# A hybrid decoder trunk on one core: output product added by halves, five column steps moved behind the first scores, key digits in one batch, first gather issued alone

## The chip, the cores and the metric

The kernel runs on 1 core of one Trainium2 chip. The metric is the device time of one execution in microseconds (us), median over runs.

## The reference, cut to what matters

```python
DEPTH, SEQ, D_MODEL = 2, 256, 1024
PEER_HEADS, PEER_TOPK, N_KEYS = 8, 16, 128
for layer in range(DEPTH):
    h = rms_norm(x, norm_mix[layer])
    z = h @ w_in[layer]                     # 1024 x 2564 columns
    ...                                     # four groups of heads: forgetting, dilated,
    ...                                     # differential attention, S5 state space model
    x = x + mixed @ w_out[layer]            # "the output product"
    h = rms_norm(x, norm_ffn[layer])
    q = (h @ wq).reshape(c, 8, 2, 128)      # queries
    sc = einsum('thpd,hpkd->thpk', q, keys) # scores against 128 keys, two sides
    top_v, top_i = top_k(sc, 16)            # per head and side
    cand = top_v[..., 0, :, None] + top_v[..., 1, None, :]      # 256 pairs
    best_v, best_pos = top_k(cand, 16)
    ids = 128 * top_i[side 0][best_pos >> 4] + top_i[side 1][best_pos & 15]
    act = gelu(einsum('td,thkd->thk', h, peer_u[ids])) * softmax(best_v)
    x = x + einsum('thk,thkd->td', act, peer_v[ids])
```

For each of 256 tokens, 128 rows of `peer_u` and 128 of `peer_v` are fetched by number in each layer.

## The kernel before, in words

The 256 tokens are two blocks of 128, and there are two layers, so the work is four passes n = 0 to 3 (layer n // 2, block n % 2). A pass has the mixing part (columns of `w_in`, heads, S5, output product, queries, scores, search for the best pairs) and the part that gathers. Each pass gathers 128 slots: slot t is one indirect DMA of GpSimd (L1724) that brings for each of 128 tokens one row of 2048 float32, the row of u and of v side by side: 1.05 MB. 512 slots in all are 538 of the 630 MB moved.

The gathered rows land in `ring`, which has 10 places. Work goes in groups of four slots. For group i VectorE makes four dot products ("dots", L1301), ScalarE a gelu, VectorE the weights ("weigh", L1310), ScalarE four diagonal matrices (L820), and TensorE four products that sum the rows of v in PSUM ("rows of v", L1669). When TensorE has used a slot (`v_used`), GpSimd may gather the next one into the same place.

The mixing part of pass n + 1 is spread between the groups of pass n. A list of names (`plan_steps`) sets the order of all steps; each engine walks that same list and does its own share of each step, in that order, with semaphores between engines. Before the first group of pass 0 stands the list `first`: there the mixing part of pass 0 has nothing to hide behind.

Names in `first` that the change touches. "out 0" to "out 3" are the output product (L1614). "out" on VectorE adds it to x (L1160). "rows 1" transposes x (L1371) and scales it into `hT` (VectorE L940 for one half, ScalarE L666 for the other). "query 4" and "score 4" are the first half of the queries and scores of quarter 0, from which "quick 0" on VectorE finds the first eight slots' ids (L1169 to L1189) and releases GpSimd by `quick_ready`. "best", "pairs" and "ids" are the full search; "ids" turns positions into row numbers (L1264 to L1286). "query 5", "query 1", "query 2" and "query 3" follow on TensorE (L1636). "next columns 0" to "7" are eight steps of the columns of block 2 (pass 1), 512 and 256 columns wide (L1434). Their input lies in ring places 4 to 6, so a gather to these places waits for `z_ps` of 8, the last of them. The weights of queries 1, 2 and 3 lie in places 8 and 9, 0 and 1, 2 and 3; so slots 4, 6 and 8 (with 5, 7 and 9 behind them) wait for `qT_ps`, the queries. Slot 10 and all later ones wait for `v_used`.

The heads, the S5 scan ("turn on"), "y" (L1573, L1574), "gate rows" (L1581) and "glu" (L1588) come ahead of the output product.

Of the kernel before, what the change touches and what calls it, by code (L numbers as in the profile page):

```python
# [8 lines left out]
ALU = mybir.AluOpType  # L9
# [6 lines left out]
P = 128  # L16
D = 1024
# [21 lines left out]
FIRST_PLACE = 4  # L39
# [92 lines left out]
def plan_steps():  # L132
# [32 lines left out]
    def do(names, n):  # L165
        for name in names:
# [3 lines left out]
            else:  # L170
# [18 lines left out]
             ["next columns 6", "rows 1", "next columns 7", "next z", "square 1", "gain", "query 4", "mean 1", "score 4"],  # L189
             ["quick 0", "best 4", "pairs 4", "query 5", "score 5", "query 1", "score 1", "ids 4", "query 2", "score 2", "best 5", "pairs 5",]]  # L190
# [49 lines left out]
def trunk(nc, x_in, w_in, w_out, row_in, gain_ffn, s5_in, glu_w, peer_wq, keys_t, table_uv,  # L240
          rel_bias, const_in, bucket_in, out):
    ctx = ExitStack()
    with ctx:
# [87 lines left out]
        posf, idf = T[:, 640:768], [T[:, 768:896], T[:, 896:1024]]  # L331
# [3 lines left out]
        hit = T[:, 2048:2560].rearrange("p (n k a) -> p n k a", k=TOPK, a=TOPK)  # L335
        v16_kept, i16_kept = by(last_keys[:, 0:64], TOPK), by(last_keys[:, 64:128].bitcast(U32), TOPK)
        late_cand = by(T[:, 4096:4352], 2 * P)
        late_hit = T[:, 4608:4864].rearrange("p (n k a) -> p n k a", k=TOPK, a=TOPK)
        late_best, late_pos = by(T[:, 4864:4896], TOPK), by(T[:, 4896:4928].bitcast(U32), TOPK)
        late_posd, late_posf, late_i16f = T[:, 4928:4960].bitcast(U32), T[:, 4960:4992], by(T[:, 4992:5056], TOPK)  # L340
        late_idf = [T[:, 5056:5088], T[:, 5088:5120]]
# [62 lines left out]
        gain_ps, mT_ps, mT_dve, mT_act, wo_ps, x_ready = sem("gain_ps"), sem("mT_ps"), sem("mT_dve"), sem("mT_act"), sem("wo_ps"), sem("x_ready")  # L404
        head_q_ps, head_qT, head_sc, cst_rest = sem("head_q_ps"), sem("head_qT"), sem("head_sc"), sem("cst_rest")
# [423 lines left out]
        def _(v):  # L829
# [326 lines left out]
            def out_rows(n, i):  # L1156
                if i == 3:
                    b = n % NB
                    v.wait_ge(wo_ps, n + 1)
                    v.tensor_tensor(x[:, b, :], x[:, b, :], ps[:, 2:4, :].rearrange("p c n -> p (c n)"), ALU.add).then_inc(x_ready, 1)  # L1160

            def quick(n, i):
# [3 lines left out]
                slots, hits = slice(0, 8), hit[:, 0, 0:8, 0:8]  # L1166
# [4 lines left out]
                for k in range(2):  # L1171
                    step.free(v.max_index(i16[:, k, 0:8], v16[:, k, 0:8], scores[k]))
                step(v.tensor_tensor(by(sums, 8), bc(v16[:, 0, 0:8], 2, 8), bc(v16[:, 1, 0:8], 1, 8), ALU.add))
                step(v.max(best[:, 0, 0:8], sums))
                step.free(v.tensor_copy(i16f[:, 0:2, 0:8], i16[:, 0:2, 0:8]))
                step(v.max_index(pos[:, 0, 0:8], best[:, 0, 0:8], sums))
                pos_f = pos.rearrange("p n k -> p (n k)")[:, slots]
                for s in range(2):
                    if s == 0:
                        step(v.tensor_single_scalar(posd[:, slots], pos_f, 3, op=ALU.logical_shift_right))  # L1180
                    else:
                        step(v.tensor_single_scalar(posd[:, slots], pos_f, 7, op=ALU.bitwise_and))
                    step(v.tensor_copy(posf[:, slots], posd[:, slots]))
                    step(v.tensor_tensor(hits, bc(posf[:, slots], 2, 8), bc(cst[:, C_IOTA:C_IOTA + 8], 1, 8), ALU.is_equal))
                    step(v.tensor_tensor(hits, hits, bc(i16f[:, s, 0:8], 1, 8), ALU.mult))
                    step(v.reduce_sum(idf[s][:, slots], hits, AX))
                step(v.scalar_tensor_tensor(out=idf[0][:, slots], in0=idf[0][:, slots], scalar=float(NK), in1=idf[1][:, slots],
                                            op0=ALU.mult, op1=ALU.add))
                v.tensor_copy(ids[:, 0, slots], idf[0][:, slots]).then_inc(quick_ready, 1)  # L1189
                v.wait_ge(quick_ready, 1)  # L1190
# [60 lines left out]
            def find_ids(n, i):  # L1251
# [9 lines left out]
                hits = hit[:, 0:count, :, :]  # L1261
                hit3 = hits.rearrange("p n k a -> p (n k) a")
# [563 lines left out]
```

## Time and profile before

| | us |
|---|---|
| median of 3 runs | 1578.69 (1577.34 to 1579.03) |
| the profiled execution's own time | 1583.69 |
| its span | 1581.9 |

In the profile, PE is TensorE's matmuls, PEld its weight loads, DVE VectorE, ACT ScalarE, POOL GpSimd, SP SyncE. A row of the timeline gives start, length, engine, line, what it writes and reads, how many instructions were merged, and in brackets the idle time before it with what ended it. PEclk is the granted TensorE clock as a share of full speed. GB/s is what the DMA engines moved in a stretch.

### The profile page before, as it was taken

To read this page: it belongs to the slowest core of one execution; us is meant where nothing else is said; L and a number is where in the kernel's file an instruction comes from. 1 tells how busy PE (TensorE), PEld (TensorE's weight loads), DVE (VectorE), ACT (ScalarE), POOL (GpSimd) and SP (SyncE) were. 2 spreads that over 40 slices of the span, in tenths; PEclk is the share of its full clock that TensorE was granted. 3 is DMA by queue.
4 is the path that set the end of the run, shared out by engine and by line. 5 is a ranking of instruction groups with operands and counts; after the bars stand their busy time and mean duration, and the time that the engine had idled before them with its cause. 6 is when DMAs were issued, how large, how long until landed. Compare 5 with 4: busy or idle time off the path is not lost.

```text
span 1581.9 us, 15174 instructions
## 1 busy us (share of the span) xinstructions
PE 1366.8 (86%) x4622; PEld 741.3 (47%) x4622; DVE 1173.6 (74%) x2848; ACT 455.0 (29%) x1095; POOL 608.3 (38%) x525
## 2 busy tenths in 40 slices
PE   8998999999695997988888799999969787788777
PEld 4766455554472444443356345455437433333333
DVE  6828999788698887874569788886658987665554
ACT  3522144443212234342122134343212222121112
POOL 1003355345334334553434333545434434333331
PEclk9999999999898999998989899999989889989999
DMA  9648999999999999999999999999999999999997
GB/s 360 269 164 347 389 380 422 406 402 421 423 421 421 422 398 422 422 419 423 423 410 409 422 423 420 417 384 403 422 423 419 388 408 422 422 419 421 422 421 300
DMA packets 87517, 629.97 MB, mean 398 GB/s; under 512 B 9825, under 2 KB 11105, under 8 KB 16910
## 3 DMA queue, kind: packets, MB, share of 16 engines
q0 software_dynamic: 74144, 537.97, 82.6%
q1 hardware_dynamic: 13294, 91.05, 14.1%
q8 instruction: 38, 0.62, 0.2%
q14 instruction: 41, 0.34, 0.1%
HBM read 627.91 MB, written 1.06 MB: 398 GB/s over the span
## 4 chain that ended last, share of the span: by engine, by line
PE 43%; DMA 29%; DVE 18%; issue 7%; ACT 3%; POOL 1%; SPq 0%; DVEq 0%; ACTq 0%
DMA ring<-table_uv,ids 28%; PE ps L1669 24%; DVE ring L1301 6%; PE ps L1636 5%; PE ps L1449 3%; PE ps L1412 2%; PE ps L1614 1%; ACT acts L797 1%; ACT diag L820 1%; PE ps L1516 1%; PE ps L1680 1%; POOL ring L1724 1%; DVE W L1276 1%; DVE W L1274 1%; DVE W L1277 1%
## 5 line engine op out<-in xcount | busy, mean ns | idle before, releaser
L1669 PE MATMUL ps<-ring,diag 128*128 128x512 f32 x1884 | 890.0, 627 | 194.3 <-ACT diag L820 185.4
L1724 POOL DMA_INDIRECT ring<-table_uv,ids x512 | 602.7, 1177 | 939.1 <-PE ps L1669 779.4
L1669 PEld LDWEIGHTS ps<-ring,diag 128*128 128x128 f32 x1884 | 370.7, 201 | 663.6 <-issue 652.0
L1301 DVE CUSTOM_DVE_ANT_0 ring<-ring,h 128x1024 f32<-128x1024 f32 x384 | 455.2, 1223 | 139.9 <-DMA ring<-table_uv,ids 137.9
L797 ACT ACTIVATE acts<-dots,small 128x4 f32<-128x4 f32 x126 | 37.5, 297 | 876.3 <-DVE dots L1301 850.3
L1301 DVE CUSTOM_DVE_ANT_0 ring<-ring,ps 128x1024 f32<-128x1024 f32 x120 | 144.6, 1220 | 97.7 <-DMA ring<-table_uv,ids 97.5
L820 ACT ACTIVATE diag<-cst,weights 128x128 f32<-128x128 f32 x471 | 151.4, 390 | 28.9 <-DVE weights L1310 27.8
L1449 PE MATMUL ps<-W,hT 128*128 128x512 f32 (+2 forms) x256 | 95.2, 527 | 2.7 <-DVE hT L940 2.7
L1636 PEld LDWEIGHTS ps<-hT,W 128*128 128x128 f32 x832 | 94.5, 192 | 3.3 <-issue 3.3
L1636 PE MATMUL ps<-hT,W 128*128 128x128 f32 x832 | 95.3, 275 | 0.0
L1449 PEld LDWEIGHTS ps<-W,hT 128*128 128x128 f32 x256 | 48.5, 190 | 52.0 <-issue 47.4
L1614 PE MATMUL ps<-W,hT 128*128 128x512 f32 x128 | 57.3, 593 | 0.8 <-DVE hT L1154 0.8
L797 ACT ACT_TABLE_LOAD x43 | 55.2, 1283 | 4.8 <-DVE dots L1301 4.0
L1310 DVE TENSOR_TENSOR weights<-acts,gates 128x4 f32<-128x4 f32 x126 | 20.6, 163 | 47.4 <-ACT acts L797 46.3
L1317 DVE SCALAR_TENSOR_TENSOR x<-ring,weights,x 128x1024 f32<-128x1024 f32 x33 | 42.4, 1285 | 1.4 <-DVE weights L1310 0.2
L1301 DVE DVE_READ_ACCUMULATOR2_ANT dots<- 128x1 f32 x504 | 41.2, 82 | 0.0
L1614 PEld LDWEIGHTS ps<-W,hT 128*128 128x128 f32 x128 | 23.9, 190 | 29.2 <-issue 28.2
L1516 PE MATMUL ps<-W 128*128 128x256 f32 (+1 forms) x128 | 32.9, 340 | 2.8 <-DVE h L1121 1.4
L1089 DVE TENSOR_REDUCE small<-ps 128x4 f32<-128x512 f32 (+1 forms) x16 | 15.3, 953 | 23.0 <-PE ps L1523 11.6
L728 ACT ACTIVATE W<-ps,small 128x128 f32<-128x128 f32 (+1 forms) x64 | 26.0, 418 | 15.4 <-DVE small L1090 15.3
L1516 PEld LDWEIGHTS ps<-W 128*128 128x128 f32 x128 | 22.2, 198 | 8.3 <-issue 5.8
L1526 PE MATMUL ps<-bias,cst 128*128 128x128 f32 (+1 forms) x96 | 24.6, 339 | 0.0
(316 smaller groups left out, 1190.8 us busy)
## 6 DMA issues: line engine op xcount, KB each, us to landing
W<-peer_wq SPq DMA_DIRECT2D x11, 2048.0 KB, 19.7
W<-w_in SPq DMA_DIRECT2D x16, 1282.0 KB, 11.6
W<-w_out SPq DMA_DIRECT2D x7, 2048.0 KB, 11.2
ring<-table_uv,ids POOLq DMA_INDIRECT x512
W<-w_in SPq DMA_DIRECT2D x8, 898.0 KB, 8.8
ring<-peer_wq SPq DMA_DIRECT2D x3, 2048.0 KB, 21.0
W<-w_in SPq DMA_DIRECT2D x4, 1024.0 KB, 11.5
ring<-w_in SPq DMA_DIRECT2D x2, 1544.0 KB, 20.3
```

The source lines that it names most:

```text
L728: a.activation(pbuf[:, i, 0:nk], lg[:, i * nk:(i + 1) * nk], ACT.Exp, bias=small[:, 72 + i:73 + i], accum_out=small[:, 80 + i:81 + i]).the ...
L797: a.activation(acts[:, g * RING_G:(g + 1) * RING_G], dots[:, g * RING_G:(g + 1) * RING_G], ACT.Gelu_apprx_tanh, scale=ffn_rstd[n % NB]).th ...
L820: a.activation(diag[:, s, :], ident, ACT.Copy, scale=weights[:, s:s + 1]).then_inc(diag_ready, 1)
L1301: v.tensor_tensor_reduce(ring_u[:, r, :], ring_u[:, r, :], tokens, 1.0, 0.0, ALU.mult, ALU.add, dots[:, s:s + 1]).then_inc(dots_done, 1)
L1317: v.scalar_tensor_tensor(out=x[:, b, :], in0=ring_v[:, r, :], scalar=weights[:, s:s + 1], in1=x[:, b, :], op0=ALU.mult, op1=ALU.add).then_ ...
L1412: mm = pe.matmul(ps[:, z_bank(0, bank), 0:c1 - c0], hT[:, k, :], first_at[group][:, k, a0:a0 + c1 - c0], start=(k == 0), stop=(k == KC - 1))
L1449: mm = pe.matmul(ps[:, 2 + i, 0:c1 - c0], hT[:, k, :], win_at(n)[:, slot, c0:c1], start=(k == 0), stop=(k == KC - 1))
L1516: pe.matmul(dst, q, k, start=True, stop=False)
L1614: mm = pe.matmul(ps[:, 2 + c, :], hT[:, k, :], half[:, k % 4, c * 512:(c + 1) * 512], start=(k == 0), stop=(k == KC - 1))
L1636: mm = pe.matmul(ps[:, 6 + q % 2, i * P:(i + 1) * P], wq_at(n, q)[:, k, i * P:(i + 1) * P], hT[:, k, :], start=(k == 0), stop=(k == KC - 1))
L1669: mm = pe.matmul(ps[:, c, :], diag[:, s, :], ring_v[:, r, c * 512:(c + 1) * 512], start=(k == 0), stop=(k == SLOTS - 1), skip_group_check= ...
L1724: gp.indirect_dma_start(ring[:, place(t), :], None, table_uv, bass.IndirectOffsetOnAxis(ap=ids[:, b, k:k + 1], axis=0)).then_inc(pair_in[p ...
```

## The change

Five things. First, in pass 0 the last step of the output product does its two chunks of 512 columns one after the other. VectorE adds each half to x when it is there (`wo_half`, `x_half`), TensorE transposes the first four blocks of x after the first half, `rows_half` releases VectorE's scaling, and the first query starts on `hT`'s first half. Second, "next columns 3" to "7" and "next z" move behind "score 4"; "next columns 2" moves to where 4 was. Third, both digits of a position (side 0 and side 1) are made by one batch of instructions of double width, in "quick" and in all "ids" steps. Fourth, the id of slot 0 is written as soon as the best key of each side is known, and its gather goes to place 7, which waits only for `glu_ps`. Fifth, other slots of the first four wait for the second increment of `quick_ready` and for `z_ps` as before.

```diff
-FIRST_PLACE = 4
+PLACES = (7, 4, 5, 6, 8, 9, 0, 1, 2, 3)
...
-             ["keys 2", "next columns 2", "weights 2", "heads 1", "next columns 3", "inverse 2"],
+             ["keys 2", "weights 2", "heads 1", "inverse 2"],
              ["heads 2", "logits 6", "co sums"],
-             ["logits 7", "y 0", "next columns 4", "softmax 3", "co scale"],
-             ["weights 3", "y 1", "next columns 5", "s5 out", "inverse 3"],
+             ["logits 7", "y 0", "next columns 2", "softmax 3", "co scale"],
+             ["weights 3", "y 1", "s5 out", "inverse 3"],
...
-             ["next columns 6", "rows 1", "next columns 7", "next z", "square 1", "gain", "query 4", "mean 1", "score 4"],
-             ["quick 0", "best 4", "pairs 4", "query 5", "score 5", "query 1", "score 1", "ids 4", "query 2", "score 2", "best 5", "pairs 5",]]
+             ["rows 1", "square 1", "gain", "query 4", "mean 1", "score 4"],
+             ["quick 0", "next columns 3", "next columns 4", "next columns 5", "next columns 6", "next columns 7", "next z", "best 4", "pairs 4", "query 5", "score 5", "query 1", "score 1", "ids 4", "query 2", "score 2", "best 5", "pairs 5",]]
...
+                    if n == 0:
+                        v.wait_ge(wo_half, 1)
+                        v.tensor_tensor(x[:, b, 0:512], x[:, b, 0:512], ps[:, 2, :], ALU.add).then_inc(x_half, 1)
+                        v.wait_ge(wo_ps, 1)
+                        v.tensor_tensor(x[:, b, 512:D], x[:, b, 512:D], ps[:, 3, :], ALU.add).then_inc(x_ready, 1)
+                        return
...
+                v.scalar_tensor_tensor(out=ids[:, 0, 0:1], in0=i16f[:, 0, 0:1], scalar=float(NK), in1=i16f[:, 1, 0:1],
+                                       op0=ALU.mult, op1=ALU.add).then_inc(quick_ready, 1)
...
-                for s in range(2):
-                    if s == 0:
-                        step(v.tensor_single_scalar(posd[:, own], pos_f, 4, op=ALU.logical_shift_right))
-                    else:
-                        step(v.tensor_single_scalar(posd[:, own], pos_f, TOPK - 1, op=ALU.bitwise_and))
-                    step(v.tensor_copy(posf[:, own], posd[:, own]))
-                    step(v.tensor_tensor(hit3, bc(posf[:, own], 2, TOPK),
-                                         bc(cst[:, C_IOTA:C_IOTA + TOPK], 1, TOPK * count), ALU.is_equal))
-                    step(v.tensor_tensor(hits, hits, bc(i4[:, :, s, :], 2, TOPK), ALU.mult))
-                    step(v.reduce_sum(idf[s][:, own], hit3, AX))
...
+                step.free(v.tensor_single_scalar(digit[:, :, 0, :], at, 4, op=ALU.logical_shift_right))
+                step(v.tensor_single_scalar(digit[:, :, 1, :], at, TOPK - 1, op=ALU.bitwise_and))
+                step(v.tensor_copy(posf[:, two], posd[:, two]))
+                step(v.tensor_tensor(hit3, bc(posf[:, two], 2, TOPK), bc(cst[:, C_IOTA:C_IOTA + TOPK], 1, 2 * TOPK * count), ALU.is_equal))
+                step(v.tensor_tensor(hits, hits, bc(i16f[:, keys, :], 2, TOPK), ALU.mult))
+                step(v.reduce_sum(idf[:, two], hit3, AX))
...
+                if n // NB:
+                    step(v.tensor_scalar(low, low, float(NE * (n // NB)), None, ALU.add))
+                v.scalar_tensor_tensor(out=dst, in0=high, scalar=float(NK), in1=low, op0=ALU.mult, op1=ALU.add).then_inc(ids_ready, 1)
...
+                order = [(k, c) for k in range(OUT_CUTS[i], OUT_CUTS[i + 1]) for c in range(2)]
+                if n == 0 and i == 3:
+                    order.sort(key=lambda kc: kc[1])
...
+                        if n == 0 and part[0] == 0 and part[-1] == 1 and (i, k) == (0, KC // 2):
+                            pe.wait_ge(rows_act, 8)
...
+                        if t == 1:
+                            gp.wait_ge(quick_ready, 2)
...
                         elif t == 0:
+                            gp.wait_ge(glu_ps, 1)
+                        elif t == 1:
                             gp.wait_ge(z_ps, 8)
```

TensorE, from the output product (L1614 before, L1633 in the changed kernel) to the second half of the first queries. In the kernel before (L1434 is a column step's two products, L1371 the transposes of x, L1636 queries, L1652 scores):

```order
L1614 MATMUL ps<-W,hT 128x512 x12
L1434 MATMUL ps<-ring,diag 128x512
L1434 MATMUL ps<-ring,diag 128x256
L1371 MATMUL ps<-cst,x 128x128 x8
L1434 MATMUL ps<-ring,diag 128x512
L1434 MATMUL ps<-ring,diag 128x256
L1636 MATMUL ps<-hT,W 128x128 x16
L1652 MATMUL ps<-key_rows,h 128x128 x2
```

The same place in the changed kernel, where column steps are L1451, transposes L1388, queries L1660 and scores L1676:

```order
L1633 MATMUL ps<-W,hT 128x512 x12
L1388 MATMUL ps<-cst,x 128x128 x8
L1660 MATMUL ps<-hT,W 128x128 x16
L1676 MATMUL ps<-key_rows,h 128x128 x2
L1451 MATMUL ps<-ring,diag 128x512
L1451 MATMUL ps<-ring,diag 128x256
```

The two column steps left the way to the first scores, and behind those scores the last pair of rows stands five times in a row before the queries go on.

VectorE, the search for the first slots' ids ("quick"). In the kernel before, from the digit of side 0 to the ids:

```order
L1180 TENSOR_SCALAR W<-W 128x8
L1183 CAST W<-W 128x8
L1184 TENSOR_TENSOR W<-W,cst 128x8x8
L1185 TENSOR_TENSOR W<-W 128x8x8
L1186 TENSOR_REDUCE W<-W 128x8
L1182 TENSOR_SCALAR W<-W 128x8
```

The same search in the changed kernel, from the end of the search in the two score lists:

```order
L1185 CAST W<-W 128x2x8
L1186 SCALAR_TENSOR_TENSOR ids<-W 128x1
L1188 TENSOR_TENSOR W<-W 128x64
L1189 MAX W<-W 128x8
L1190 MAX_INDEX W<-W 128x8
L1192 TENSOR_SCALAR W<-W 128x8
L1193 TENSOR_SCALAR W<-W 128x8
L1194 CAST W<-W 128x16
L1196 TENSOR_TENSOR W<-W,cst 128x128
L1197 TENSOR_TENSOR W<-W 128x128
L1198 TENSOR_REDUCE W<-W 128x16
L1199 SCALAR_TENSOR_TENSOR ids<-W 128x7
```

The id of slot 0 is now written second of these rows, and the cast, compare, multiply and sum that stood once for each side stand once.

GpSimd, its first gathers with their waits, in the kernel before:

```order
L1724 DMA ring<-table_uv,ids 128x2048 [waits z_ps,quick_ready]
L1724 DMA ring<-table_uv,ids 128x2048 x3
L1724 DMA ring<-table_uv,ids 128x2048 [waits qT_ps]
```

And in the changed kernel:

```order
L1752 DMA ring<-table_uv,ids 128x2048 [waits glu_ps,quick_ready]
L1752 DMA ring<-table_uv,ids 128x2048 [waits z_ps,quick_ready]
L1752 DMA ring<-table_uv,ids 128x2048 x2
L1752 DMA ring<-table_uv,ids 128x2048 [waits qT_ps]
```

The first gather no longer waits for the column steps; the second one does.

## Rows read from the trace of the kernel before

**Rows 1.** The page's span and DMA total.
```profile
span 1581.9 us, 15174 instructions
DMA packets 87517, 629.97 MB, mean 398 GB/s; under 512 B 9825, under 2 KB 11105, under 8 KB 16910
```

**Rows 2.** Stretches: length, busy us (count) per engine, granted clock, DMA share, GB/s.
```profile
78.00:82.00 4.00, 4.00 (x16) 2.74 (x15) 1.31 (x5) 2.52 (x9) 0.00 (x0) 0.57 0.00 0
160.00:175.00 15.00, 12.70 (x30) 5.44 (x30) 14.39 (x54) 1.57 (x5) 8.77 (x7) 1.00 0.90 334
212.00:224.00 12.00, 12.00 (x31) 5.50 (x31) 11.15 (x23) 7.96 (x15) 7.58 (x6) 1.00 0.81 300
285.00:360.00 75.00, 69.33 (x256) 40.33 (x255) 61.37 (x145) 34.34 (x77) 33.22 (x27) 0.95 1.00 403
360.00:580.00 220.00, 189.48 (x664) 103.53 (x663) 179.83 (x476) 51.32 (x117) 88.78 (x72) 0.94 1.01 422
580.00:600.00 20.00, 19.52 (x54) 9.53 (x53) 18.88 (x45) 12.73 (x25) 8.47 (x7) 1.00 0.93 375
1240.00:1300.00 60.00, 43.16 (x80) 18.07 (x81) 53.55 (x159) 12.96 (x33) 22.74 (x22) 0.83 0.99 390
```

**Rows 3.** Timeline of GpSimd: slots 0, 1, 8, 14 and 30.
```profile
117.39 1.02 POOL L1724 DMA_INDIRECT ring<-table_uv,ids  x1 [96.49 <-DVE ids L1189]
118.71 0.97 POOL L1724 DMA_INDIRECT ring<-table_uv,ids  x1 [0.30 <-issue]
...
143.06 0.94 POOL L1724 DMA_INDIRECT ring<-table_uv,ids  x1 [5.51 <-PE ps L1636]
...
160.21 0.94 POOL L1724 DMA_INDIRECT ring<-table_uv,ids  x1 [7.59 <-PE ps L1669]
...
214.40 1.75 POOL L1724 DMA_INDIRECT ring<-table_uv,ids  x1 [6.74 <-PE ps L1669]
```

**Rows 4.** Timeline of TensorE, from the heads to the first rows of v.
```profile
71.05 1.51 PE L1434 MATMUL ps<-ring,diag 128*128 128x512 f32 x4
72.39 1.00 PE L1563 MATMUL ps<-zkv,W 128*128 128x64 f32 x8
...
75.78 0.49 PE L1516 MATMUL ps<-W 128*128 128x128 f32 x2 [1.44 <-DVE h L1121]
...
93.07 10.46 PE L1614 MATMUL ps<-W,hT 128*128 128x512 f32 x24
103.37 1.45 PE L1434 MATMUL ps<-ring,diag 128*128 128x512 f32 x4
...
107.28 3.81 PE L1636 MATMUL ps<-hT,W 128*128 128x128 f32 x32
...
112.17 3.74 PE L1636 MATMUL ps<-hT,W 128*128 128x128 f32 x32
...
143.97 6.60 PE L1669 MATMUL ps<-ring,diag 128*128 128x512 f32 x15
```

**Rows 5.** Timeline of VectorE: adds, searches, digits, and dots of group 1.
```profile
73.76 1.23 DVE L1079 TENSOR_TENSOR W<-W 128x1024 f32<-128x1024 f32 x1
...
103.57 1.22 DVE L1160 TENSOR_TENSOR x<-x,ps 128x1024 f32<-128x1024 f32 x1 [13.98 <-PE ps L1614]
...
112.37 0.50 DVE L1169 MAX8 W<-ps 128x8 f32<-128x128 f32 x2 [2.77 <-PE ps L1652]
...
122.40 0.17 DVE L1270 TENSOR_SCALAR W<-W 128x16 uint32<-128x16 uint32 x1
...
122.81 0.43 DVE L1274 TENSOR_TENSOR W<-W,cst 128x256 f32<-128x256 f32 x1
...
126.59 0.17 DVE L1284 TENSOR_REDUCE small<-gates 128x1 f32<-128x16 f32 x1
...
150.58 1.23 DVE L1301 CUSTOM_DVE_ANT_0 ring<-ring,h 128x1024 f32<-128x1024 f32 x1
...
183.21 0.69 DVE L1274 TENSOR_TENSOR W<-W,cst 128x512 f32<-128x512 f32 x1
```

More of the change, by code:

```diff
@@ L1165, in quick @@
                 sums = cand[:, 0, 0:64]
-                slots, hits = slice(0, 8), hit[:, 0, 0:8, 0:8]
+                slots, two = slice(0, 8), slice(0, 16)
+                hits = hit[:, 0:128].rearrange("p (s k a) -> p s k a", s=2, k=8)
+                digit = posd[:, two].rearrange("p (s k) -> p s k", s=2)
                 v.wait_ge(head_sc, 1)
@@ L1187, in quick @@
[L1187 to L1190, printed above, removed]
+                step.free(v.tensor_single_scalar(digit[:, 0, :], pos_f, 3, op=ALU.logical_shift_right))
+                step(v.tensor_single_scalar(digit[:, 1, :], pos_f, 7, op=ALU.bitwise_and))
@@ new lines, in quick @@
+                step(v.tensor_copy(posf[:, two], posd[:, two]))
+                hit3 = hits.rearrange("p s k a -> p (s k) a")
+                step(v.tensor_tensor(hit3, bc(posf[:, two], 2, 8), bc(cst[:, C_IOTA:C_IOTA + 8], 1, 16), ALU.is_equal))
+                step(v.tensor_tensor(hits, hits, bc(i16f[:, 0:2, 0:8], 2, 8), ALU.mult))
+                step(v.reduce_sum(idf[:, two], hit3, AX))
+                v.scalar_tensor_tensor(out=ids[:, 0, 1:8], in0=idf[:, 1:8], scalar=float(NK), in1=idf[:, 9:16],
+                                       op0=ALU.mult, op1=ALU.add).then_inc(quick_ready, 1)
@@ L1278, in find_ids @@
-                step(v.scalar_tensor_tensor(out=idf[0][:, own], in0=idf[0][:, own], scalar=float(NK), in1=idf[1][:, own],
-                                            op0=ALU.mult, op1=ALU.add))
-                step(v.tensor_scalar(idf[0][:, own], idf[0][:, own], float(NE * (n // NB)), None, ALU.add))
-                rest = slice(8, TOPK) if i == 4 else part
-                v.tensor_copy(ids[:, b, rest], idf[0][:, own if late else rest]).then_inc(ids_ready, 1)
+                at = by(pos_f, TOPK)
@@ L1283, in find_ids @@
+                step(v.reduce_sum(idf[:, two], hit3, AX))
+                k0 = 8 if i == 4 else 0
+                dst = by(ids[:, b, part], TOPK)[:, :, k0:TOPK]
+                high, low = found[:, :, 0, k0:TOPK], found[:, :, 1, k0:TOPK]
+                if n // NB:
+                    step(v.tensor_scalar(low, low, float(NE * (n // NB)), None, ALU.add))
+                v.scalar_tensor_tensor(out=dst, in0=high, scalar=float(NK), in1=low, op0=ALU.mult, op1=ALU.add).then_inc(ids_ready, 1)
                 v.wait_ge(gate_exp, found_ids(n, i))
@@ L1610, in out_rows @@
                     pe.wait_ge(wout_low_load, 16 * (n + 1))
-                for k in range(OUT_CUTS[i], OUT_CUTS[i + 1]):
-                    half = wout_halves[k // 4]
-                    for c in range(2):
+                order = [(k, c) for k in range(OUT_CUTS[i], OUT_CUTS[i + 1]) for c in range(2)]
+                if n == 0 and i == 3:
+                    order.sort(key=lambda kc: kc[1])
+                for k, c in order:
+                        half = wout_halves[k // 4]
                         mm = pe.matmul(ps[:, 2 + c, :], hT[:, k, :], half[:, k % 4, c * 512:(c + 1) * 512], start=(k == 0), stop=(k == KC - 1))
+                        if n == 0 and (k, c) == (KC - 1, 0):
+                            mm.then_inc(wo_half, 1)
                 if i == 3:
```

50 lines of the change are left out of this document (28 added, 22 removed).

## The prediction

> **What bounds the kernel now.** I read the total first. The span moves 630 MB [rows 1], and in a long undisturbed stretch the DMA engines move 422 GB/s (360 to 580 [rows 2]). 630 MB at 422 GB/s are 1493 us of a span of 1581.9. So the time is these 1493 us plus the time in which the DMA engines move less than they could, 89 us. An edit can save time only if it takes away some of this shortfall; an edit that shortens an engine's work while DMA is full buys nothing.
>
> Then the stretches. The shortfall of a stretch is its length times (1 - GB/s / 422). It is 3.1 us at 160 to 175, 3.5 us at 212 to 224, 3.4 us at 285 to 360, 2.2 us at 580 to 600 and 4.6 us at 1240 to 1300 [rows 2]. The rest lies before 160 or at the very end.
>
> Third, the timeline of GpSimd. The first gather starts at 117.39, when "quick" has written its ids, and slot 1 at 118.71. But slot 8 starts only at 143.06, released by the queries (L1636), and by then DMA had run dry. Slots 14 and 30 start at 160.21 and 214.40, both after a wait for TensorE's products of the rows of v (L1669) of 7.59 and 6.74 us [rows 3]. These two waits are the shortfalls at 160 to 175 and 212 to 224. In them VectorE is busy 14.39 of 15 us and 11.15 of 12, and TensorE all of the 12 [rows 2]. So from about 143 to 224 the engines are late and DMA waits for them; before 143 the slots wait for the queries.
>
> This gives two clocks to keep. The **DMA clock** is when slot 8 can start, since what was gathered before it has landed. The **engine clock** is when VectorE and TensorE do their groups. The later of the two sets the gathers up to 224.
>
> **The change part by part.**
>
> Up to the end of the output product (103.53 = 93.07 + 10.46 [rows 4]). Column steps leave TensorE here: a step costs 1.34 us, from 71.05 to 72.39 [rows 4]. Steps 3 and 2 leave a place where VectorE is the one waited for: the next logits on TensorE start at 75.78 after 1.44 us of idle time, released by VectorE [rows 4]. They save nothing there. Step 5 stood ahead of the last heads and saved time is possible, about 1 us. Against it stands the clock. It already falls, to a mean of 0.57 at 78 to 82 [rows 2], that is to the lower level of 1.2 GHz for most of that stretch, right after those 1.44 us of idle time, and the change makes that idle time about 1.3 us longer. A lower clock some 3 us earlier would slow the logits and "y", both on the way, by 1 to 2 us. Between -1.0 and +1.0 us, I take **0**.
>
> The Trainium skill ("TensorE: Matmul & The Clock Gate", Part 1) says that the idle state is the throttled one and that activity releases it, which speaks against taking matmuls out of a thin stretch; the trace agrees in that the only low clock between 60 and 104 comes behind the idle time. By the page alone this term would be +1.
>
> From the end of the product to the first scores: 112.37 - 103.53 = 8.84 us today [rows 4, 5]. In it lie the add of 1.22 us, eight transposes, the scaling and 3.81 us of queries [rows 4, 5]. New: the first half's add is done under the last products. The second half's add, of half the width, costs 0.69, by the row of 512 elements [rows 5]; it starts 0.05 after the product, and the first four transposes lie under it. From there: the other transposes 0.55, ScalarE's four scalings 1.15, then 28 of 32 query instructions, 3.81 × 28/32 = 3.3, less the first four that are waited for (24 of 32: 2.85), and 1.28 from the queries' end to the scores' use (112.37 - 107.28 - 3.81). Sum 0.05 + 0.7 + 0.6 + 1.2 + 2.85 + 1.28 = 6.7. Saved: **2.2 us**. The bounds are the removed half add alone (0.5) and all of the add and half the scaling (3).
>
> Five column steps now stand between "score 4" and "query 5": 5 × 1.34 = **6.7 us** on TensorE. Two of them had been covered, by VectorE's add and by the scaling; two or three by VectorE's scan. Nothing covers them now, because query 5 started at 112.17 [rows 4], at the very time of the scores. Queued behind them are queries 5, 1, 2 and 3, and slots 4 to 9 wait for these. So the DMA clock moves by 6.7 - 2.2 + 0 = **+4.5 us** (slot 8 from 143.06 to 147.6). Low end 3.5, high end 5.5 by the term above. The early gathers buy nothing: slot 0 starts some 5.3 us earlier than today, since "quick" writes it 1.6 us after its start where all eight took 5.0 (117.39 - 112.37 [rows 3, 5]), and slots 1 to 3 wait for the last column step, at about 117. Both are dry long before slot 8.
>
> The engine clock. VectorE: scores 2.2 earlier. "quick" loses four small instructions and two of 64 elements become one of 128: 0.7. "ids 4" takes from 122.40 to 126.59, 4.19 us [rows 5]. New: two digits and a cast at 0.2, less an overlap of 0.1, three instructions of 512 elements at 0.69 + 0.04 instead of six of 256 at 0.43 + 0.03, one ending instruction at 0.2 instead of three: 2.9. Saved 1.3, and 1.3 again in "ids 5". Group 1's dots, at 150.58 today [rows 5], can so start 5.5 us earlier; its four slots, 4 to 7, land 4.5 later than today, at about 146, which still fits. So group 1 is weighed some 5 us earlier. TensorE: the rows of v of group 0 move from 143.97 [rows 4] to 148.5, those of group 1 can follow without a gap, at about 156.4, and slot 14 is released near 158. DMA, with slots 8 to 13 in hand, runs dry at 160.2 + 4.5 = 164.7. **No shortfall at 160 to 175: -3.1.** TensorE then goes on without a gap, about 4.0 us ahead of today, because VectorE's group 2 ends 5 us ahead and its row scaling waits less. So slot 30 is released at 210.4. DMA, now 4.5 - 3.1 = 1.4 us behind today, runs dry at about 215. **No shortfall at 212 to 224: -3.5.** Sum by 224: +4.5 - 6.6 = -2.1.
>
> Later passes. An "ids" step with two heads changes six instructions of 512 elements (0.69 + 0.03) into three of 1024 (1.23 + 0.03 [rows 5]) and loses two or three small ones: 1.1 to 1.3 us each, 12 such steps. Where DMA is full that is nothing. It counts where DMA falls short and VectorE is late. At 1240 to 1300 VectorE is busy 53.6 of 60 us [rows 2], with two ids steps in it or right before: -1.4. At 580 to 600 TensorE is busy 19.5 of 20, so little: -0.3. At 285 to 360 the two late steps lie near the end: -0.3. Sum **-2.0**, between 0 (if the shortfalls are TensorE's) and -4.
>
> Total: 4.5 - 6.6 - 2.0 = **-4.1 us**. The sum is made against the profiled execution, 1583.69 (its span and 1.8 us around it), which stands 5.0 above the median of the runs; I carry the difference over to the median: 1578.69 - 4.1 = **1574.6**.
>
> **The rivals.** About 0.2% (3.2 us) is what this measurement can tell from no change.
>
> *A. The forecast*, the late start paid back by full DMA afterwards: 1574.6, chance 0.48.
>
> *B. The second shortfall stays.* TensorE has no gap at 212 to 224 [rows 2], so it alone could hold slot 30, if its lead is used up by waits on late slots. Then 4.5 - 3.1 - 2.0 = -0.6: 1578.1. For it: TensorE's own start of the rows of v is 4.5 us later. Against: the gap ahead of group 1 is longer than that. Chance 0.24.
>
> *C. Slower: the late queries are not paid back.* The place is slots 4 to 9. If the dots of groups 1 and 2 then wait for slots that land 4.5 us later, the releases of slots 14 and 30 move later with them, and both shortfalls stay: +4.5 - 1 (ids) = +3.5, 1582.2. It decides once less than 1.3 us of the 6.6 comes back. Against it: VectorE is busy 14.39 of 15 us at 160 to 175, so it is work and not arrivals that it is late by. Chance 0.13.
>
> *D. More.* The output product comes 1 us earlier, the clock holds, and the lead over DMA also closes part of 285 to 360 (2 of 3.4): 3.5 - 6.6 - 4.2 = -7.3, 1571.4. Chance 0.15.
>
> **How the numbers follow.** A's own range is 1572.5 to 1576.5. The range over all reaches to D and stops short of the worst of C: 1570.8 to 1580.0. Faster by over 0.2% is below 1575.5: most of A (0.38) and D (0.15), 0.53. Slower by over 0.2% is above 1581.9: half of C and a tail, 0.11. The rest, 0.36, is no change.
>
> **What would show it.** In the changed kernel's profile: slot 0 near 112 and slot 1 near 117; slot 8 near 147.5 (DMA clock); 422 GB/s from there past 224 with no dip at 160 to 175 and 212 to 224; group 1's dots near 145; clock below 1 some 3 us earlier than at 78 (the term of 0). It would be wrong if slot 8 comes later than 149, which means another TensorE wait behind the columns, or if GpSimd still waits some 6 us for slots 14 and 30 with DMA dry.

## The result, and the profile after

The changed kernel is slower: median of 5 runs 1587.19 us (1583.19 to 1592.63), against 1578.69 (1576.12 to 1580.8) for the kernel before in the same session. The ratio is 1.0051, with a 95% interval of 1.0033 to 1.007. Predicted were 1574.6 us and a range of 1570.8 to 1580.0. Two runs of more than 3500 us in the last set of experiments (one of the kernel before, one of the kernel before with both ids early) are in the medians of the table below and not in its ratios.

The profiled execution of the changed kernel took 1583.7 us, near the lowest of its runs; one that was profiled later took 1585.81. The kernel before was profiled at 1583.69, five above its median. So the two spans are equal by chance, and the stages must be read one by one. The page, its span and DMA totals, which answer to [rows 1]:

```profile
span 1581.9 us, 15072 instructions
DMA packets 87516, 629.97 MB, mean 398 GB/s; under 512 B 9825, under 2 KB 11105, under 8 KB 16910
```

The stretches of [rows 2] in the changed kernel, with the same columns:

```profile
78.00:82.00 4.00, 4.00 (x26) 3.20 (x26) 0.09 (x1) 2.34 (x6) 0.00 (x0) 0.81 0.00 0
160.00:175.00 15.00, 12.69 (x28) 5.25 (x28) 14.32 (x60) 1.57 (x5) 7.28 (x6) 0.95 0.90 341
212.00:224.00 12.00, 12.00 (x32) 5.57 (x31) 10.19 (x19) 7.10 (x14) 6.79 (x5) 1.00 0.83 328
285.00:360.00 75.00, 70.40 (x263) 41.07 (x262) 61.27 (x137) 35.60 (x80) 33.85 (x29) 0.98 1.00 406
580.00:600.00 20.00, 20.00 (x57) 9.93 (x56) 18.65 (x46) 13.48 (x28) 7.28 (x6) 1.00 0.93 359
1240.00:1300.00 60.00, 45.63 (x90) 19.03 (x91) 53.05 (x155) 12.96 (x33) 25.45 (x24) 0.89 1.00 400
```

Both dips that were to vanish are there: 341 GB/s at 160 to 175 is still 2.9 us short of 422, and 328 at 212 to 224 is 2.7 us short. GpSimd's timeline, the slots of [rows 3] and slot 1:

```profile
109.34 1.02 POOL L1752 DMA_INDIRECT ring<-table_uv,ids  x1 [88.29 <-DVE ids L1186]
114.69 0.97 POOL L1752 DMA_INDIRECT ring<-table_uv,ids  x1 [4.34 <-PE ps L1451]
...
144.63 0.94 POOL L1752 DMA_INDIRECT ring<-table_uv,ids  x1 [5.51 <-DVE ids L1293]
...
161.86 0.94 POOL L1752 DMA_INDIRECT ring<-table_uv,ids  x1 [7.66 <-PE ps L1693]
...
215.98 1.75 POOL L1752 DMA_INDIRECT ring<-table_uv,ids  x1 [6.81 <-PE ps L1693]
```

Slots 8, 14 and 30 are all later than in [rows 3], by 1.57, 1.65 and 1.58 us. From slot 8 on, the whole pattern has moved by one amount, that of the queries. TensorE, answering to [rows 4]:

```profile
71.04 0.39 PE L1543 MATMUL ps<-bias,cst 128*128 128x128 f32 x2
73.75 0.49 PE L1533 MATMUL ps<-W 128*128 128x128 f32 x2 [2.32 <-DVE h L1124]
...
90.07 10.46 PE L1633 MATMUL ps<-W,hT 128*128 128x512 f32 x24
...
107.29 6.62 PE L1451 MATMUL ps<-ring,diag 128*128 128x512 f32 x20
113.75 3.73 PE L1660 MATMUL ps<-hT,W 128*128 128x128 f32 x32
...
157.93 8.80 PE L1693 MATMUL ps<-ring,diag 128*128 128x512 f32 x16 [4.49 <-ACT diag L820]
```

The last row is the rows of v of group 1. They still wait 4.49 us for ScalarE's diagonals, as in the kernel before; the prediction had this gap gone. The row of before:

```profile
156.36 8.80 PE L1669 MATMUL ps<-ring,diag 128*128 128x512 f32 x16 [4.49 <-ACT diag L820]
```

Why it stayed is seen on VectorE ("ids 4", answering to [rows 5]) and on ScalarE at the same time:

```profile
107.50 0.50 DVE L1180 MAX8 W<-ps 128x8 f32<-128x128 f32 x2 [2.81 <-PE ps L1676]
...
116.50 0.17 DVE L1278 TENSOR_TENSOR gates<-W 128x16 f32<-128x16 f32 x1
...
119.63 0.17 DVE L1293 SCALAR_TENSOR_TENSOR ids<-W 128x8 uint32<-128x8 f32 x1
128.16 0.17 DVE L1295 TENSOR_REDUCE small<-gates 128x1 f32<-128x16 f32 x1 [8.36 <-ACT gates L783]
...
152.16 1.22 DVE L1312 CUSTOM_DVE_ANT_0 ring<-ring,h 128x1024 f32<-128x1024 f32 x1
```

```profile
125.91 0.60 ACT L776 ACTIVATE zkv<-ps 128x512 f32<-128x512 f32 x1 [8.01 <-PE ps L1660]
126.52 1.28 ACT L783 ACT_TABLE_LOAD   x1
127.82 0.31 ACT L783 ACTIVATE gates<-gates,small 128x16 f32<-128x16 f32 x1
```

VectorE writes the input of the exponential (L783) at 116.50 and has all ids at 119.8. But the exponential stands in ScalarE's order behind the copy of query 1 (L776), and that copy waits until TensorE has made query 1, at 125.9. So VectorE stands still for 8.36 us, and everything behind, the second search and the dots of group 0 among it, starts at a time that the queries set. The last row of VectorE is the first of group 1's dots: 152.16, where the kernel before has 150.58 [rows 5] and the prediction near 145. The Trainium skill ("PSUM — Partial Sum Buffer", Engine vs sequencer instructions) calls ScalarE's queue strictly first in, first out; the trace agrees, with 11.3 us from the input to the exponential. In the kernel before, the same exponential ran at 126.25:

```profile
126.25 0.31 ACT L783 ACTIVATE gates<-gates,small 128x16 f32<-128x16 f32 x1
```

There VectorE came for it at 126.59 [rows 5], just as it ended, and had no wait.

### The profile page after: what moved, and what is told of

It reads as the page before. It is cut to its first block, busy times and chain, and to the rows that moved or that the text cites. A ratio compares the mean times of both kernels' runs of the same rounds, so it can differ in the third digit from the quotient of the medians.

```text
span 1581.9 us, 15072 instructions
## 1 busy us (share of the span) xinstructions
PE 1359.9 (86%) x4622; PEld 737.2 (47%) x4622; DVE 1155.5 (73%) x2745; ACT 455.0 (29%) x1095; POOL 603.7 (38%) x525
## 2 busy tenths in 40 slices
DMA packets 87516, 629.97 MB, mean 398 GB/s; under 512 B 9825, under 2 KB 11105, under 8 KB 16910
## 4 chain that ended last, share of the span: by engine, by line
PE 48%; DMA 28%; DVE 14%; issue 6%; ACT 2%; POOL 1%; SPq 0%; DVEq 0%; ACTq 0%
PE ps L1693 28%; DMA ring<-table_uv,ids 27%; PE ps L1466 6%; PE ps L1660 5%; DVE ring L1312 5%; PE ps L1633 2%; DMA ring<-w_in 1%; PE ps L1429 1%; ACT acts L797 1%; ACT diag L820 1%; PE ps L1533 1%; PE ps L1704 1%; PE ps L1543 1%; PE ps L1451 1%; POOL ring L1752 1%
## 5 line engine op out<-in xcount | busy, mean ns | idle before, releaser
L1312 DVE CUSTOM_DVE_ANT_0 ring<-ring,ps 128x1024 f32<-128x1024 f32 x120 | 144.8, 1221 | 100.4 <-DMA ring<-table_uv,ids 100.1
L1660 PEld LDWEIGHTS ps<-hT,W 128*128 128x128 f32 x832 | 94.6, 192 | 3.5 <-issue 2.9
L1660 PE MATMUL ps<-hT,W 128*128 128x128 f32 x832 | 95.5, 275 | 0.2 <-ACT hT L666 0.2
L1633 PE MATMUL ps<-W,hT 128*128 128x512 f32 x128 | 57.3, 593 | 0.8 <-DVE hT L1157 0.8
L1633 PEld LDWEIGHTS ps<-W,hT 128*128 128x128 f32 x128 | 23.9, 190 | 29.2 <-issue 28.2
## 6 DMA issues: line engine op xcount, KB each, us to landing
W<-w_in SPq DMA_DIRECT2D x4, 1024.0 KB, 11.5
```

Of the source, the lines that this page charges most:

```text
L1312: v.tensor_tensor_reduce(ring_u[:, r, :], ring_u[:, r, :], tokens, 1.0, 0.0, ALU.mult, ALU.add, dots[:, s:s + 1]).then_inc(dots_done, 1)
L1633: mm = pe.matmul(ps[:, 2 + c, :], hT[:, k, :], half[:, k % 4, c * 512:(c + 1) * 512], start=(k == 0), stop=(k == KC - 1))
L1660: mm = pe.matmul(ps[:, 6 + q % 2, i * P:(i + 1) * P], wq_at(n, q)[:, k, i * P:(i + 1) * P], hT[:, k, :], start=(k == 0), stop=(k == KC - 1))
```

## The experiments

All were timed beside the kernel before, whose median was 1579.2 in the first four runs, 1579.3 in the next four and 1579.8 in the last three. The three sets ran on three chips, so kernels of different sets are compared through the kernel before. Two theories: **clock**, the columns' leaving makes TensorE's clock fall for longer; **lock**, VectorE is tied to the queries through ScalarE's queue, so that a late query is never paid back. The rival to both is that the move costs only its own 6.5 us on TensorE.

| kernel | median, us | ratio (95%) | end of product | query 5 | slot 8 | slot 14 | 8 to 14 |
|---|---|---|---|---|---|---|---|
| before | 1579.2 | 1 | 103.5 | 112.2 | 143.1 | 160.2 | 17.1 |
| changed, first profile | 1587.2 | 1.0051 (1.0033 to 1.007) | 100.5 | 113.8 | 144.6 | 161.9 | 17.2 |
| changed, again | 1586.7 | 1.0057 (1.0042 to 1.0071) | 105.6 | 118.8 | 149.7 | 166.7 | 17.0 |
| column steps put back | 1576.8 | 0.999 (0.9978 to 1.0001) | 100.7 | 108.8 | 139.7 | 157.1 | 17.3 |
| "ids 4" early | 1584.7 | 1.0034 (1.0021 to 1.0047) | 106.4 | 119.7 | 150.6 | 167.9 | 17.3 |
| before, columns moved | 1589.8 | 1.0061 (1.0046 to 1.0076) | 109.3 | 124.4 | 155.3 | 172.0 | 16.7 |
| fillers | 1582.9 | 1.0016 (1.0004 to 1.0029) | 103.8 | 117.1 | 147.9 | 165.3 | 17.3 |
| both ids early | 1578.7 | 0.9987 (0.9968 to 1.0006) | 106.8 | 120.0 | 150.9 | 161.7 | 10.8 |
| columns back, both ids early | 1576.4 | 0.9976 (0.9963 to 0.9988) | 100.8 | 108.9 | 139.8 | 151.3 | 11.5 |
| digits alone | 1578.6 | 0.9994 (0.9977 to 1.001) | 103.4 | 112.0 | 142.9 | 160.0 | 17.1 |
| fillers, both ids early | 1578.1 | 0.9993 (0.9976 to 1.0009) | 100.7 | 113.9 | 144.8 | 155.6 | 10.8 |
| before, both ids early | 1579.6 | 0.9997 (0.9982 to 1.0012) | 100.3 | 109.0 | 139.9 | 156.2 | 16.3 |
| halves taken out | 1577.8 | 0.9986 (0.9968 to 1.0004) | 100.6 | 109.3 | 140.2 | 157.5 | 17.3 |

The ratio is estimated from the single runs and can differ from the quotient of the medians by 0.001. The times of stages are from the one profiled execution of each.

**The changed kernel again.**

> The changed kernel once more, to size the loss in other runs than the first five. Theory S (the loss is real and comes from the start: TensorE's column steps put queries 5, 1, 2 and 3 and so slots 4 to 9 later by 1.6 us, and VectorE is held to the same lateness by the wait for ScalarE's exponential behind query 1): the two profiles differ by 1.7 us of DMA shortfall at 240 us, so a ratio of about 1.001 to 1.002. Theory L (something in the later passes is slower too): 1.005 again, with most of the shortfall after 240 us. Theory N (the five runs fell high by chance): within 0.1% of before.

1586.7 us, the result repeated. Its profile has a low clock for much longer: added up over windows of 1 us, 13.6 us at 0.50, where the first profile has 3.4. Windows of 4 us from 74:

```profile
74.00:78.00 4.00, 3.71 (x18) 3.71 (x18) 3.37 (x11) 1.95 (x5) 0.00 (x0) 0.50 0.00 0
78.00:82.00 4.00, 4.00 (x12) 2.82 (x12) 0.43 (x2) 1.05 (x6) 0.00 (x0) 0.50 0.00 0
82.00:86.00 4.00, 4.00 (x29) 3.86 (x27) 0.51 (x2) 1.99 (x3) 0.00 (x0) 0.75 0.00 0
86.00:90.00 4.00, 3.42 (x14) 2.58 (x13) 0.85 (x2) 2.20 (x4) 0.00 (x0) 0.67 0.83 274
```

The granted clock is 0.50, 1.2 GHz, from 74 to 82, though TensorE is busy nearly all the time, and below full speed until past 90. The output product ends at 105.6, 5.0 later than in the first profile of the same kernel; the logits had begun 0.5 later (74.30 for 73.75), and the rest came with the clock.

**Only the column steps put back** in the lists:

```diff
-["keys 2", "weights 2", "heads 1", "inverse 2"]
+["keys 2", "next columns 2", "weights 2", "heads 1", "next columns 3", "inverse 2"]
...
-["quick 0", "next columns 3", "next columns 4", "next columns 5", "next columns 6", "next columns 7", "next z", "best 4", ...
+["quick 0", "best 4", ...
```

> The changed kernel with only the five column steps (and next z) put back where they were. Theory S: everything from slot 4 on starts about 3 to 5 us earlier than before (output product 0 to 1 earlier, halves 1.8, no 6.5 us of columns ahead of query 5), slot 8 near 140 to 141, and the time is 2 to 4 us under before and 4 to 8 under the changed kernel. Theory L: slot 8 as early, but the time stays 3 or more us above before, since digits, places or halves cost it later on.

1576.8 us, 9.9 less than the changed kernel beside it. The same windows:

```profile
74.00:78.00 4.00, 4.00 (x28) 3.21 (x28) 3.27 (x10) 2.40 (x7) 0.00 (x0) 1.00 0.00 0
78.00:82.00 4.00, 3.44 (x24) 2.86 (x24) 0.51 (x2) 2.89 (x7) 0.00 (x0) 1.00 0.00 0
82.00:86.00 4.00, 3.23 (x22) 2.57 (x20) 1.10 (x3) 2.12 (x4) 0.00 (x0) 1.00 0.91 303
86.00:90.00 4.00, 3.51 (x8) 1.58 (x9) 0.77 (x2) 0.24 (x1) 0.00 (x0) 1.00 0.91 340
```

The clock is full throughout. Slot 8 starts 10.0 us earlier than in the changed kernel run beside it. The medians differ by 9.9, the two profiled executions by 8.7. The loss is the placement of the column steps, and it is 3.4 us more than their own 6.5 us on TensorE, which goes against the rival. By the profiles, 4.9 of the 10.0 us stand at the end of the product, where only the clock and the columns' places differ, and 5.1 come between it and query 5.

**"ids 4" ahead of "query 1"** in the list, in the changed kernel:

```diff
-... "query 5", "score 5", "query 1", "score 1", "ids 4", "query 2", ...
+... "query 5", "score 5", "ids 4", "query 1", "score 1", "query 2", ...
```

> The changed kernel with ids 4 put before query 1 in the list, so that ScalarE's exponential for the gates no longer stands behind the copy of query 1, for which it waited from 117.9 to 125.9. Theory S says this wait is why VectorE gained no lead: its idle 8.4 us at 119.8 to 128.2 goes, group 1's dots start near 146 and not 152, slots 14 and 30 no longer wait with DMA dry, and the time falls by 4 to 6 us against the changed kernel. Rival (the releases of slots 14 and 30 hang on TensorE or on late slots): VectorE starts earlier, waits later, and the time falls by under 1.5 us.

1584.7 us, 2.0 below the changed kernel where 4 to 6 were expected. Slot 8 to slot 14 stayed at 17.3 us. "ids 5" has the same wait, behind the copy of query 3. It was 1.76 us in the first profile (at 146.14); here, with "ids 4" open, it is longer:

```profile
152.08 0.17 DVE L1295 TENSOR_REDUCE small<-gates 128x1 f32<-128x16 f32 x1 [5.78 <-ACT gates L783]
```

So the time won at the first lock was lost at the next, and one of two locks was open.

**The kernel before with only the column steps moved.**

> The kernel before with only the column steps moved. Theory S: query 5 starts 3 to 4 us later than before (no halves to pay for it), slot 8 near 146, time +2 to +4 us over before. Theory L (columns are not what costs): within 1.5 us of before.

1589.8 us, 10.6 above before, where 2 to 4 were expected. In its profile the clock was 0.50 in each window read from 74 to 94, and 0.50 or little more up to 98. This is the loss of the move without the other four parts.

**Fillers.** Two idle steps on TensorE, of three products of 256 columns, where column steps 2 and 3 stood. They begin a new sum in block 2's columns, so part of block 2's columns, and with it the kernel's result, is changed in this kernel and in the later one with fillers; the bytes moved are the same 629.97 MB.

```diff
-["keys 2", "weights 2", "heads 1", "inverse 2"]
+["keys 2", "fill 0", "weights 2", "heads 1", "fill 1", "inverse 2"]
...
+            def fill(n, i):
+                for r in range(3):
+                    pe.matmul(ps[:, 1, 256:512], next_hT[:, 6, :], first_at[2][:, 6, 0:256], start=True, stop=True, skip_group_check=True)
```

> The changed kernel with two idle fillers of three products (256 columns wide) each on TensorE at the places where column steps 2 and 3 stood; their results go to an unused part of PSUM. The way to the first scores gets no useful work back, and the five column steps stay ahead of query 5. Theory K (the clock): in the changed kernel TensorE's 2.3 us of idle time ahead of 74 drops the granted clock for 10 to 24 us over the output product's way, which costs some 4 us; with the fillers the clock drops for 3.4 us at most between 70 and 100 and the time falls by 4 to 6 us against the changed kernel, to 1 to 3 us over before. Rival R (the columns' own time ahead of query 5 is what costs): no more than 1 us falls.

1582.9 us, 3.8 less than the changed kernel (4 to 6 were expected), for products that add nothing but work; the intervals of the two ratios do not meet. The windows:

```profile
74.00:78.00 4.00, 3.97 (x28) 3.36 (x28) 3.41 (x11) 2.22 (x7) 0.00 (x0) 1.00 0.00 0
78.00:82.00 4.00, 3.44 (x28) 3.18 (x26) 0.51 (x2) 2.90 (x8) 0.00 (x0) 0.90 0.00 0
82.00:86.00 4.00, 3.53 (x12) 2.66 (x13) 0.57 (x2) 1.84 (x3) 0.00 (x0) 0.50 0.85 295
86.00:90.00 4.00, 3.22 (x9) 1.78 (x8) 1.30 (x3) 0.80 (x2) 0.00 (x0) 0.50 0.88 289
```

The clock leaves 1.00 one window later than in the changed kernel run again, and is at 0.50 only from 82. So the clock is part of the cost. In this profile the fall was put off and not prevented. No filler stood where column step 5 had been, just before 81, and whether one there would have held the clock was not tried.

**Both ids steps freed**, in the changed kernel: "ids 4" as above, and

```diff
-                do(["query 3", "score 3"], n)
+                do(["ids 5", "query 3", "score 3"], n)
...
-    inner = [["ids 5", "best 1"], ...
+    inner = [["best 1"], ...
```

> The changed kernel with both of ScalarE's exponentials freed: ids 4 before query 1 and ids 5 before query 3 in the list. In all runs so far TensorE idles 4.49 us ahead of the rows of v of group 1, whatever else changes. Theory Q (that gap is the chain query 3, copy on ScalarE, table load, exponential of ids 5, VectorE's gates, best 1, dots 1): the gap shrinks by some 5 us, VectorE's dots 1 come up to 8 us earlier against query 3's end, the shortfall between 145 and 224 falls by 3 to 6 us, and the time falls 3 to 5 us under the changed kernel. Rival (landing of slots 4 to 7 holds dots 1): VectorE waits on DMA instead and less than 2 us are gained.

1578.7 us, 8.5 below the changed kernel's first median and 8.0 below the second, though slot 8 is as late as ever (150.92). That is more than the 3 to 5 expected. The profiled execution was one of its longer ones, 1581.92, and its runs spread from 1573 to 1589 us. VectorE, GpSimd and TensorE in this kernel:

```profile
125.92 0.17 DVE L1293 SCALAR_TENSOR_TENSOR ids<-W 128x8 uint32<-128x8 f32 x1
126.00 0.16 DVE L1295 TENSOR_REDUCE small<-gates 128x1 f32<-128x16 f32 x1
```

```profile
150.92 0.94 POOL L1752 DMA_INDIRECT ring<-table_uv,ids  x1 [7.32 <-PE ps L1660]
...
161.73 0.94 POOL L1752 DMA_INDIRECT ring<-table_uv,ids  x1 [1.19 <-PE ps L1693]
```

```profile
151.83 7.03 PE L1693 MATMUL ps<-ring,diag 128*128 128x512 f32 x16
158.70 1.04 PE L1388 MATMUL ps<-cst,x 128*128 128x128 f32 x8
159.57 7.03 PE L1693 MATMUL ps<-ring,diag 128*128 128x512 f32 x16
```

The wait of 8.36 us is gone, group 1's rows of v follow without the 4.49, and slot 14 comes 10.8 us after slot 8 where it came 17. A third tie of the same kind is still there: the gelu of group 0 stands behind the copy of query 2, and VectorE's "weigh" waits 6.15 us for it, where it waited 1.70 in the first profile. What opening it would give was not tried.

```profile
141.19 0.60 ACT L776 ACTIVATE h<-ps 128x512 f32<-128x512 f32 x1 [8.39 <-PE ps L1660]
```

```profile
143.43 0.16 DVE L1321 TENSOR_TENSOR weights<-acts,gates 128x4 f32<-128x4 f32 x1 [6.15 <-ACT acts L797]
```

The stretches:

```profile
160.00:175.00 15.00, 12.14 (x25) 5.07 (x24) 14.32 (x62) 2.55 (x9) 6.53 (x6) 0.89 1.02 424
212.00:224.00 12.00, 12.00 (x33) 5.79 (x32) 8.21 (x16) 4.99 (x11) 4.35 (x4) 1.00 0.87 342
```

The first dip has vanished as the prediction had it. The second has not: 342 GB/s, 2.3 us short, with TensorE busy all 12 us. This is rival B's point: the gather of slot 30 waits 6.81 us for TensorE there, as in the changed kernel.

**Columns back and both ids freed**; halves, digit batch and early gather kept.

> The candidate: column steps back in their old places, halves, digit batch and first gather kept, both exponentials freed. Theory Q plus K: 3 to 6 us under before (1573 to 1576), the clock not below full between 60 and 100, and DMA's shortfall at 145 to 224 smaller by 3 to 6 us than in the kernel before. Rival: as the kernel with the columns back alone, 1 to 3 us under before.

1576.4 us: 0.9976 (0.9963 to 0.9988), the only one of these kernels whose interval lies clear below 1, and so faster than both given kernels. From "columns back" to this the gain is 0.4 in the medians, inside the noise. Against "both ids early" it gives what the moved columns cost without the lock: 1578.7 - 1576.4 = 2.3 us, of the 9.9 with it. The intervals of the two ratios overlap, so the 2.3 may be less; that it is not 9.9 is clear of noise. Its dip at 160 to 175 is gone as well, but part of it comes back later: 200 to 224 runs at 350 GB/s, where the kernel before has 356.

```profile
160.00:175.00 15.00, 14.83 (x33) 6.95 (x34) 14.29 (x57) 3.76 (x10) 4.34 (x4) 0.89 1.02 422
200.00:224.00 24.00, 24.00 (x83) 12.88 (x82) 18.18 (x40) 13.24 (x25) 12.45 (x10) 1.00 0.90 350
```

**The digit batch alone**, in the kernel before.

> The kernel before with the digits of a position in one batch and nothing else of weight (quick keeps one tiny extra instruction for slot 0, and the gather waits for all eight ids). VectorE's busy total falls by some 17 us. My term for this is -2.0 us in later passes plus up to 0.5 from quick. Rival (VectorE is covered everywhere that DMA is short, or held by ScalarE's queue): within 0.1%.

1578.6 us, nothing that can be told from no change, though VectorE's busy time falls from 1173.6 us in the page of before to 1153.7. Page of this kernel, busy time of each engine:

```profile
PE 1362.5 (86%) x4622; PEld 739.3 (47%) x4622; DVE 1153.7 (73%) x2744; ACT 455.3 (29%) x1095; POOL 605.5 (38%) x525
```

**Three to close.** Fillers and both ids together:

> The changed kernel with the column steps still behind the first scores, with idle filler products where column steps 2 and 3 stood, and with both ids steps ahead of the query copies that held VectorE. If the clock (some 4 us) and the wait in ScalarE's queue (some 8 us) are two separate costs, this comes to 1587 - 4 - 8 = 1575 us. If they are one cost seen twice (a slow clock only mattered since the queries were waited for), it stays at the 1578.7 us of the kernel with both ids steps moved and no filler.

1578.1 us against 1578.7 without fillers. They do not add up to the 1575 of two separate costs, which lies below the interval: by the medians, clock and lock are largely one loss. A slow clock makes the queries late, and the lock passes that on to everything behind. The two profiled executions do not fit this so well: here the clock was low for 3.4 us, slot 8 came at 144.8 and the time was 1575.2; without fillers it was low for 17.1 us, slot 8 came at 150.9 and the time was 1581.9. So how much of a late slot 8 still reaches the end with both locks open is not settled.

The kernel before with both ids steps freed:

> The kernel before with nothing but both ids steps moved ahead of the query copies. If that wait cost only what the late queries made of it, this gains 0 to 1 us: 1578 to 1579. If the wait was a cost of its own in the kernel before as well, it gains a good part of the shortfall of 3 us at 160 to 175: 1575.5 to 1577.

1579.6: no gain. With queries as early as they were, the lock cost nothing that can be told: the exponential of "ids 4" was just in time, as the row at 126.25 shows. Nor does slot 14 come much sooner, 16.3 us after slot 8, and with the digit batch alone it comes after 17.1; with both, in the kernel with columns back, it comes after 11.5. So it looks as if the batch's saving on VectorE shows only when the locks are open, and the open locks only when VectorE is ahead.

The changed kernel with columns back and the halves taken out:

> The changed kernel with the column steps put back and the output product added to x in one piece again; the digits in one batch and the early first gather stay. If the 2 us that the halves take off the way to the first scores reach the end, this is 2 us slower than with them: 1578.5 to 1579. If they don't, it is 1576.8 like the kernel with the halves.

1577.8, ratio 0.9986 against 0.999 with the halves. The 0.9 us between the medians is less than can be told apart. It is also a smaller test than was meant: with the column steps in place, the halves bring the first scores only 0.5 us nearer to the end of the product (8.3 us against 8.8, in the profiles of the two kernels), not 2.

## Why the prediction was wrong

**The method held as far as slot 8 goes.** The run moves the same 630 MB at the same mean of 398 GB/s, and slot 8's start carries to the end. In the nine profiles with at least one lock closed, slot 8 starts between 139.7 and 155.3, and the executions' own times rise with it by 0.94 us for each us, with single ones up to 3.0 us off the line. The two kernels with moved columns and both locks open lie 6.2 and 7.1 us below that line. One execution alone shows little: the two profiles of the changed kernel are 5.1 us apart at slot 8 and 2.1 at the end.

**"Up to the end of the output product ... Between -1.0 and +1.0 us, I take 0": the size was wrong.** It measured -3.0 in one profile of the changed kernel and +2.0 in the next. But the profile of before is itself a late one: its clock was at 0.50 from 47 to 51 as well as at 78 to 82, and the prediction read the clock from 60 on. The kernel before with both ids early has the same steps up to the product and, with a full clock, ends it at 100.3. Against that the term is +0.2 and +5.3. In the same way the idle time ahead of the logits grew to 2.32 us from 1.44, and from 0.82 in the undisturbed profile. I took the price of the clock as "a lower clock some 3 us earlier". It was that in the first profile, with 3.4 us at 0.50 from 76, and 13.6 us at 0.50 in the second. With the columns moved the fall was there in every profile, for 3 to 24 us; with them in place it was 3.4 us at 78 to 82 in two profiles (before, digits alone) and absent in the other four. Fillers won back 3.8 us of the median. The Trainium skill ("TensorE: Matmul & The Clock Gate", Part 1) calls the throttled clock the default that activity releases. The +1 that the prediction drew from it has the sign that these traces show against an undisturbed profile, and is too small for the second one.

**Product to first scores, -2.2:** measured 107.50 - 100.53 = 6.97 for 8.84, so -1.9. Right in size. The last experiment gives the halves 0.5 of it with the column steps in place; the other 1.4 came only with column steps 6 and 7 out of the way. Whether the 1.9 reached the total, no run shows.

**Five column steps, +6.7:** measured 113.75 - 107.29 = 6.5. Right. So the DMA clock moved by -3.0 - 1.9 + 6.5 = +1.6 in the first profile and by +2.0 - 1.9 + 6.5 = +6.6 in the second, for +4.5 predicted. Against the undisturbed profile (slot 8 at 139.9) it moved by 4.8 and 9.8.

**"Group 1's dots, at 150.58 today [rows 5], can so start 5.5 us earlier": this step failed.** I added VectorE's savings in "quick" and "ids 4" as if VectorE ran freely, and had not read ScalarE's timeline. In "ids 4" VectorE waits for an exponential that is queued behind a copy of query 1. VectorE had its ids 6.8 us earlier than in the kernel before, the copy came 1.6 later, and both together became 8.36 us of waiting. Group 1's dots started at 152.16, 1.6 later than before and not 5.5 earlier: the engine clock moved later with the queries. There were not two clocks but one, tied at the copy. The sign that the prediction had named for being wrong was there: GpSimd still waited 7.66 and 6.81 us for slots 14 and 30, with DMA short. The sum of -6.6 for the two dips was therefore 0. Freed of both locks, the same kernel gives the first dip back and nearly all of the loss, though its dots of group 1 start at 152.58, with slot 8 at 150.92.

**The second dip** would have stayed anyway, as rival B said: TensorE is busy all 12 us of it in the changed kernel as in [rows 2], and with the locks open too.

**Later passes, -2.0:** the three stretches (1240, 580 and 285) changed by -1.4, +0.8 and -0.5 us. But the digit batch alone is 0.9994 (0.9977 to 1.001); a gain of 2 us lies inside that interval and is not shown. That 20 us less work on VectorE moves the end so little fits DMA being full nearly everywhere.

**Early gathers:** slot 0 at 109.3 and slot 1 at 114.7 (112 and 117 predicted). That they bought nothing, since slot 8 sets the time, is argued and no run tests it alone.

**The outcome was rival C's kind**, late queries not paid back, at 0.13. Its condition was wrong: it expected the dots to wait for slots that land late, and its price was 1582.2. With the terms of the second profile, +6.6 and nothing back, the sum is 1585.3; the remaining 1.9 us to the median I have not placed. With those of the first, +1.6, it would be 1580.3, so the sum hangs on how long the clock was low.

## What to carry to other kernels

Before a saving on one engine is counted, look up each thing that it waits for next, and what stands ahead of that thing in the other engine's queue: a small exponential behind a PSUM copy can tie two engines that seem free. When work is moved out of a thin stretch of TensorE, price the stretch at half clock for its whole length as the worse case, not for the gap alone. And where a late step moves every later start by the same amount, there is one chain, so look for the link before forecasting that slack behind it will pay the delay back.

## What the runs showed of the hardware

TensorE's clock stayed at 0.50 for 8 us and more while the records show it busy (3.71 and 4.00 of 4 us). How long the fall lasts differs between executions of one program: the changed kernel's product ended at 100.5 and 105.6 in two profiles, and its runs spread from 1583 to 1593 us. In the kernel before the product ended at 103.5, with a clock of 0.57 at 78 to 82 and at 47 to 51. With both ids steps freed, which leaves all that stands ahead of the product as it is, it ended at 100.3 with a clock of 1.00 in both. The stretch 47 to 51, first before, then before with both ids freed:

```profile
47.00:51.00 4.00, 3.80 (x17) 3.71 (x18) 3.64 (x15) 3.08 (x10) 0.00 (x0) 0.57 1.04 442
47.00:51.00 4.00, 4.00 (x23) 2.89 (x22) 3.79 (x15) 3.08 (x7) 0.00 (x0) 1.00 0.98 418
```

Of the 3.2 us between the two, 0.7 were there before 42, at full clock in both; the other 2.5 came at and behind the two falls. Idle time alone does not foretell it: the kernels with columns back have 0.82 us ahead of the logits and a full clock, while the fillers cut the gap ahead of the logits from 2.32 to 0.81 us, and the clock fell all the same, for 10.2 us from 81 in one profile and for 3.4 us from 76 in the other. What sets the length of the fall stays open.
